# One block for the whole input projection of a hybrid decoder layer, with its guests handing memory over by semaphores

## The reference

```python
h = rms_norm(x, norm_g)
proj = jnp.einsum('btd,dn->btn', h, w_in)            # 544 rows x 7964 columns
...
xp = jnp.concatenate([buf, cqk], axis=1)             # group C: short causal convolution
for j in range(CONV_W):
    acc = acc + xp[:, j:j + T] * c_conv_w[j]
qk_c = jax.nn.silu(acc)
...
hc, (C1, n1, m1) = mlstm_chunkwise(qc, kc, vc, gif[:, :, 0], gif[:, :, 1], C0, n0, m0)
```

## Time and profile before

| what | value |
|---|---|
| three runs | 1905.7, 1909.7, 1914.8 us |
| median | 1909.7 us |
| span of the profiled execution, first to last instruction | 1913.1 us |
| time of the profiled execution | not listed apart from its span |
| TensorE busy | 1684.6 us, 88% of the span |
| granted TensorE clock, mean | 0.942 of full |
| slots 66 to 127 with their results | about 458 to 998 us |

### The profile page before, as it was taken

The page is one execution under the profiler, slowest core; times in us unless marked ns, Lnnn a source line. Parts: engine busy times, 40 slices in busy tenths (PEclk is TensorE's granted clock), DMA queues, the critical chain, the costliest instruction groups (busy, mean ns, idle before and its releaser), DMA issues. The chain is left out here.

```text
span 1913.1 us, 39025 instructions
## 1 busy us (share of the span) xinstructions
PE 1684.6 (88%) x14897; PEld 1300.9 (68%) x14897; DVE 808.4 (42%) x1592; ACT 586.3 (31%) x1353; POOL 103.8 (5%) x166
## 2 busy tenths in 40 slices
PE   6999998998998899999978887888888888369998
PEld 5888888776777677777556756666666666157776
DVE  4221222352266432334425654466455565374221
ACT  4321112231223121221115213455445455262110
POOL 3000000151000000000001000000000000020000
PEclk9999999998999999999897878999999999779999
DMA  6465555684422314124146515999999999193343
GB/s 210 154 200 184 173 188 159 220 292 127 157 70 91 110 51 127 56 83 119 47 140 238 171 41 183 358 358 384 372 384 373 374 364 378 53 332 88 122 158 115
DMA packets 218112, 373.28 MB, mean 195 GB/s; under 512 B 41917, under 2 KB 122254, under 8 KB 216614
## 3 DMA queue, kind: packets, MB, share of 16 engines
q1 hardware_dynamic: 214390, 359.24, 55.0%
q0 software_dynamic: 3248, 9.44, 1.5%
q10 hardware_dynamic: 288, 2.10, 0.3%
HBM read 334.27 MB, written 40.69 MB: 196 GB/s over the span
## 5 line engine op out<-in xcount | busy, mean ns | idle before, releaser
L370 PE MATMUL pj_ps<-pj_whi,pj_xhi 128*128 128x512 f32 (+1 forms) x1024 | 417.9, 408 | 5.9 <-PEq L86 5.9
L371 PE MATMUL pj_ps<-pj_wlo,pj_xhi 128*128 128x512 f32 (+1 forms) x1024 | 402.7, 393 | 0.0
L372 PE MATMUL pj_ps<-pj_whi,pj_xlo 128*128 128x512 f32 (+1 forms) x1024 | 401.4, 392 | 0.0
L288 DVE TENSOR_TENSOR pj_wlo<-pj_w,pj_whi 128x1024 fp32r<-128x1024 f32 (+1 forms) x128 | 156.2, 1221 | 461.1 <-ACT pj_whi L246 459.8
L246 ACT ACTIVATE pj_whi<-pj_w 128x1024 fp32r<-128x1024 f32 (+1 forms) x128 | 132.4, 1034 | 522.9 <-DMA pj_w<-in_w_in 521.5
L370 PEld LDWEIGHTS pj_ps<-pj_whi,pj_xhi 128*128 128x128 f32 x1024 | 198.3, 194 | 67.6 <-issue 30.9
L372 PEld LDWEIGHTS pj_ps<-pj_whi,pj_xlo 128*128 128x128 f32 x1024 | 198.0, 193 | 40.8
L371 PEld LDWEIGHTS pj_ps<-pj_wlo,pj_xhi 128*128 128x128 f32 x1024 | 198.8, 194 | 34.3
L1589 ACT ACTIVATE da_kT<-da_tp 128x512 f32<-128x512 f32 x200 | 119.2, 596 | 168.4 <-PE da_tp L1470 155.7
L1676 DVE COPY da_kT<-da_tp 128x512 f32<-128x512 f32 x128 | 88.5, 691 | 73.2 <-PE da_tp L1470 72.8
L3116 PE MATMUL ou_ps<-ou_whi,ou_mhi 128*128 128x512 f32 x256 | 104.7, 409 | 6.5 <-DVE ou_wlo L3040 6.5
(11 more groups left out here) (531 smaller groups left out, 2284.8 us busy)
## 6 DMA issues: line engine op xcount, KB each, us to landing
at_early_a<-in_cache_a_kv SPq DMA_DIRECT2D x128, 512.0 KB, 6.4
da_pa<-in_cache_a_kv SPq DMA_DIRECT2D x128, 512.0 KB, 6.7
pj_w<-in_w_in SPq DMA_DIRECT2D x120, 512.0 KB, 4.6
px_pages<-in_cache_b_kv SPq DMA_DIRECT2D x256, 128.0 KB, 2.5
at_early_b<-in_cache_b_kv SPq DMA_DIRECT2D x128, 128.0 KB, 6.5
da_pb<-in_cache_b_kv SPq DMA_DIRECT2D x128, 128.0 KB, 6.8
ou_w<-in_w_out SPq DMA_DIRECT2D x32, 512.0 KB, 4.3
proj<-pj_out SPq DMA_DIRECT2D x52, 256.0 KB, 5.6
```

The source lines that it names most:

```text
L288: dve.tensor_tensor(self.wlo[:, r, :, 0:n], self.w[:, r, :, 0:n], self.whi[:, r, :, 0:n], ALU.subtract).then_inc(self.wlo_ready, 1)
L370: pe.matmul(acc, hi, high, start=kc == 0, stop=False)
L371: pe.matmul(acc, hi, low, start=False, stop=False)
L372: last = pe.matmul(acc, lo, high, start=False, stop=kc == KC - 1)
```

## The change

The four blocks become one. `project` becomes the class `Opening`, whose `program` runs all 128 slots. The function `guests` strings the guests' generators together: when the beats of one segment are over, what is left of that guest is written out in one piece at the first turn of the next segment, and the next guest's turn 1 follows in the same turn. `Lease` is a stage that hands its semaphores to its owner: its memory is given back when it closes, but it clears nothing and has no barrier. Semaphores are cleared once, where the stage "pj" closes. In the place of the barriers come waits: `room` (norms stored, pages used) before the convolution's first loads and its first VectorE work, `k_copied` before the prompt part's loads and masks, and on GpSimd the landing of the prompt part's last stores before the sample part's masks. Last, the prompt part's SyncE, TensorE, ScalarE and VectorE streams start four turns later (`LEAD = 4`), except for four small copies on VectorE, so that its 72 turns are 76; and the sample part's `START` goes from 8 to 14.

```diff
+class Lease(Stage):
+    def __init__(self, nc, name, owner):
+        super().__init__(nc, name)
+        self.owner = owner
+    def sem(self, name):
+        return self.owner.sem(f"{self.name}_{name}")
...
@@ Opening.program (each engine; here SyncE) @@
                 for g in range(end):
                     a.sp_slot(sp, g)
+                part = guests(segments, "sp", sp)
+                for g in range(end, a.SLOTS):
+                    a.sp_slot(sp, g)
+                    beats(a, part, g)
+                for _ in part:
+                    pass
+                a.sp_end(sp)
...
-def hosted(nc, host, first, last, guest):
...
+def beats(host, part, g):
+    for _ in range(4 if g % host.NP < host.NP - 1 else 0):
+        next(part, None)
+
+def guests(segments, engine, eng):
+    for guest, first, last in segments:
+        part = {"sp": guest.sp, "pool": guest.pool, "act": guest.act, "dve": guest.dve, "pe": guest.pe}[engine](eng)
+        for _ in range(4 * sum(1 for g in range(first, last) if g % Projection.NP < Projection.NP - 1)):
             next(part, None)
+            yield
+        for _ in part:
+            pass
...
@@ Convolve @@
+    def room(self, eng):
+        for t in range(5):
+            eng.wait_ge(self.before.norms.stored[t], 48)
+        eng.wait_ge(self.host.pages_used, 8 * DB)
...
+        self.room(sp)
         sp.dma_start(self.old[32:36, :], d.c_conv_w).then_inc(self.w_loaded, 16)
...
+        self.room(dve)
         step(dve.memset(self.xp[:, :, 0:3], 0.0))
...
@@ PromptMemory @@
-    HEADBEATS, UNITBEATS = 15, 7
+    LEAD, HEADBEATS, UNITBEATS = 4, 15, 7
...
+        for _ in range(self.LEAD):
+            yield
+        sp.wait_ge(self.before.k_copied, 5)
         for t in range(5):
             sp.wait_ge(self.host.stored[t], (16 if t < PT else 64) * 10)
...
     def pool(self, pool):
+        pool.wait_ge(self.before.k_copied, 5)
...
     def pe(self, pe):
-        for _ in range(3):
+        for _ in range(self.LEAD + 3):
             yield
...
     def act(self, act):
-        for _ in range(3):
+        for _ in range(self.LEAD + 3):
             yield
...
         step(dve.tensor_copy(k.gates_s[:, 1, :], k.gate_f[:, SEQ:ROWS]))
+        for _ in range(self.LEAD):
+            yield
         dve.wait_ge(self.zeroed, 5)
...
@@ SampleMemory @@
-    START = 8
+    START = 14
...
     def pool(self, pool):
+        pool.wait_ge(self.before.out_stored, 16 * 7)
+        pool.wait_ge(self.before.h_stored, 16 * len(self.before.UNITS))
...
@@ stages @@
-            project(nc, d, k, host, 66)
-            with Stage(nc, "ml") as c:
+            with Lease(nc, "px", s) as g:
+                opening = Opening(nc, d, k, host, g)
+            with Lease(nc, "ml", s) as c:
...
-                    with Stage(nc, "cv") as g:
-                        hosted(nc, host, 66, 90, Convolve(nc, d, k, host, g))
-                    with Stage(nc, "mp") as g:
-                        hosted(nc, host, 90, 112, PromptMemory(nc, d, k, host, g))
-                with Stage(nc, "md") as g:
-                    hosted(nc, host, 112, 128, SampleMemory(nc, d, k, host, g))
+                    with Lease(nc, "cv", s) as g:
+                        conv = Convolve(nc, d, k, host, opening, g)
+                    with Lease(nc, "mp", s) as g:
+                        prompt = PromptMemory(nc, d, k, host, conv, g)
+                with Lease(nc, "md", s) as g:
+                    sample = SampleMemory(nc, d, k, host, prompt, g)
+            opening.program(66, [(conv, 66, 90), (prompt, 90, 112), (sample, 112, 128)])
```

More of the change, by code:

```diff
@@ L527, in dve, with __init__, program @@
             dve.tensor_scalar(ss[0:rows, t, 16:22], ss[0:rows, t, 16:22], 1.0 / HEAD, None, ALU.mult).then_inc(self.summed, 1)
-def project(nc, d, k, a, end):
-    with Stage(nc, "px") as s:
+class Opening:
+    def __init__(self, nc, d, k, a, s):
+        self.nc, self.d, self.k, self.a = nc, d, k, a
         a.pages = s.sb("pages", [P, 3, 4, 2 * HEAD])
         a.table = s.sb("table", [1, DB * PAGES], I32)
[L535 to L550, removed]
+        self.x = s.sb("x", [P, 5, D])
+        self.sq = s.sb("sq", [P, D])
+        self.ssq = s.sb("ssq", [P, 8])
+        self.rms = s.sb("rms", [P, 8])
+        self.gain = s.sb("gain", [P, KC])
+        self.xg = s.sb("xg", [P, 3, 4, P])
+        self.x_loaded = s.sems("x_loaded", 5)
+        self.gain_loaded = s.sem("gain_loaded")
+        self.made = s.sem("made")
+        self.z_zeroed = s.sem("z_zeroed")
+        self.turned = s.sem("turned")
+        self.xg_ready = s.sem("xg_ready")
+        self.xhi_ready = s.sem("xhi_ready")
+        self.squared = s.sem("squared")
+        self.rooted = s.sem("rooted")
+        self.norms = Norms(nc, d, k, a, self.x, self.sq, s)
+    def program(self, end, segments):
+        nc, d, k, a = self.nc, self.d, self.k, self.a
+        x, sq, ssq, rms, gain, xg = self.x, self.sq, self.ssq, self.rms, self.gain, self.xg
+        x_loaded, gain_loaded, made, z_zeroed = self.x_loaded, self.gain_loaded, self.made, self.z_zeroed
+        turned, xg_ready, xhi_ready = self.turned, self.xg_ready, self.xhi_ready
+        squared, rooted, norms = self.squared, self.rooted, self.norms
         parts = [(t, q) for t in range(5) for q in range(4)]
@@ L603, in _ @@
                 norms.pool(pool)
+                for _ in guests(segments, "pool", pool):
+                    pass
             @block.scalar
@@ L629, in _ @@
                     norms.act(act, g)
+                part = guests(segments, "act", act)
+                for g in range(end, a.SLOTS):
+                    a.act_slot(act, g)
+                    beats(a, part, g)
+                for _ in part:
+                    pass
             @block.vector
@@ L663, in _ @@
                         dve.wait_ge(a.rstd_ready, 1)
+                part = guests(segments, "dve", dve)
+                for g in range(end, a.SLOTS):
+                    a.dve_slot(dve, g)
+                    beats(a, part, g)
+                for _ in part:
+                    pass
             @block.tensor
@@ L683, in _ @@
                     a.pe_slot(pe, g)
+                part = guests(segments, "pe", pe)
+                for g in range(end, a.SLOTS):
+                    a.pe_slot(pe, g, part)
+                for _ in part:
+                    pass
 class Blocks:
@@ L1807, in _ @@
                     dve.tensor_copy(oo[:, 1 + x // 2, 4 * (x % 2):4 * (x % 2) + 4, :], src).then_inc(out_dve, 1)
-def hosted(nc, host, first, last, guest):
-    def beats(part, g):
-        for _ in range(4 if g % host.NP < host.NP - 1 else 0):
-            next(part, None)
[L1820 to L1861, removed]
+def beats(host, part, g):
[5 more added lines that the diff above has]
+        for _ in range(4 * sum(1 for g in range(first, last) if g % Projection.NP < Projection.NP - 1)):
+            next(part, None)
+            yield
+        for _ in part:
+            pass
 class Convolve:
@@ L1868, with __init__ @@
     N = len(JOBS)
-    def __init__(self, nc, d, k, host, s):
-        self.d, self.k, self.host = d, k, host
+    def __init__(self, nc, d, k, host, before, s):
+        self.d, self.k, self.host, self.before = d, k, host, before
         self.banks = host.ps[5:8]
@@ L2418, with __init__ @@
     V = HEAD + 1
-    START = 8
-    def __init__(self, nc, d, k, host, s):
-        self.d, self.k = d, k
+    START = 14
+    def __init__(self, nc, d, k, host, before, s):
+        self.d, self.k, self.before = d, k, before
         self.bx, self.by, self.bz = host.ps[5], host.ps[6], host.ps[7]
@@ L3177, in stages @@
                 k.gates_s = c.sb("gates_s", [HC, 2, NS])
-                with Stage(nc, "mi") as m2:
+                with Lease(nc, "mi", s) as m2:
                     k.qkT = m2.sb("qkT", [P, 8, ROWS])
```

## The result

| | before | after |
|---|---|---|
| median, 20 runs each | 1908.1 us | 1916.9 us |
| ratio after / before, 95% interval | | 1.0045 (1.0030 to 1.0061) |
| span of the profiled execution | 1913.1 us | 1917.9 us |
| TensorE busy, granted clock | 1684.6 us, 0.942 | 1685.1 us, 0.943 |
| slots 89 to 111 | 231.3 us | 238.3 us |

By the ratio the kernel is 8.6 us slower (0.45%, interval 5.7 to 11.6). That is just inside the 0.5% that I called no change, but the interval leaves out 1. The forecast was +17.4: its direction held, and about half of its size. One of the changed kernel's 20 executions took 2023.9 us at a mean clock of 0.816 and is left out of the ratio.

What follows compares the result with a forecast made beforehand. TensorE, busy 88% of the span, was taken as the bound. Barriers -7.1, LEAD +8.9, handover +8.9 and rest of the sample part +6.7 sum to +17.4 us, on the median 1909.7: 1927 us; range 1904 to 1938.

Steps and rivals of the forecast that it cites:

- the barriers' terms of 7.1: Three inner barriers and the final clear removed: 1.8, 2.95 with 1.7 of clock, and 0.6, together 7.1 us saved.
- The handover's stop: At the third barrier, slot 112 starts 1.1 us after TensorE ends slot 111 instead of 4.05: 2.95 us back.
- The 0.6 for the final clear: At the end, one semaphore clear with its barrier goes; worth 0 to 0.9 us, taken as 0.6.
- LEAD in slots 90 to 111: Prompt part four turns later: idle +6.1, clock +2.8, together +8.9 us; bounds -7.7 and +14.
- the 1.7 at turns 19 and 20: Slot 94: query scaling and two key weights wait behind the split; two stops of some 0.8, sum 1.7 us.
- The handover: Slot 112: late-landing prompt stores delay state and weight loads; idle +5.4, clock +3.5, together +8.9 us; bounds 0 and +13.
- 1.7 of clock behind the third barrier: Stretch 850 to 860 us: 3.4 us at 1.2 GHz, 1.7 us of work lost, which removing the barrier gives back.
- turn 26: Slot 118, sample part: key weights and weighing fall behind the split, a stop of 1.0 us.
- the rest of the sample part, six turns later: Turn 26 1.0, slot 120 0.5, slot 126's late weights 3.5 and clock 1.7: together +6.7 us; bounds 0 and +11.
- Leads do what a lead can: Rival: guest turns find their data ready because weights arrive earlier; -15 us, 1895 us; chance 0.10.
- In part: Rival: handover costs but VectorE's turns keep clear of splits, or the other way round; 1911 us, within 0.5%; chance 0.28.
- the same rule: VectorE is in order, so even-slot guest turns run after the split, past +6.4 us, though TensorE asks at +1.4 to +5.6.

Runs made afterwards that it cites:

- kernel 1: The changed kernel with LEAD 0 and START 8 as before the change, also called block only: ratio 0.9954 to the kernel before, median 1897.6 us.
- kernel 9: The changed kernel without its two stores of n_p, run once: 1904.2 us; SyncE's wait at the handover 2.6 us instead of 7.7.
- kernels 2 and 3: The changed kernel with START 8 and LEAD still 4: ratio 1.0047 to before; the changed kernel with LEAD 0 and START still 14: 0.9946.
- kernels 4 and 7: The changed kernel with VectorE's guest turns before the split in even slots from 90: 0.9914; that plus both store moves: 0.9872 (ratios to before).
- kernel 11: The kernel before, barriers kept, with VectorE's guest turns ahead of the low split in even slots from 90: ratio 0.9869, median 1885.9 us.

## Why the prediction was half right

The forecast's terms can be set beside the two profiles, place by place (the barriers' terms of 7.1 stand where they belong):

| place | forecast | the two profiles |
|---|---|---|
| slots 64 to 88 | -0.9 | -3.7 |
| slots 89 to 111, with the handover's stop | +5.0 | +7.0 |
| slots 112 to 126 | +13.9 | +7.8 |
| slot 127 to the next stage's first matmul | -0.6 | +0.1 |
| sum | +17.4 | +11.2 |

These are two single executions. Slot 64 starts at 445.5 us before and at 440.3 after, though the programs do the same work up to there; the thirteen kernels' profiles have it between 440 and 447. And the profile before is a slow one: its span of 1913.1 fits only the run of 1914.8 us, the slowest of the twenty (a run's time is some 1.8 us above its span).

**The barriers: -7.1 forecast, -8.8 measured** by kernel 1 (interval -5.3 to -12.0). The handover's stop is 1.16 in every kernel with one block, as worked out (1.1). The 0.6 for the final clear wasn't there: from the start of slot 127 to the next stage's first matmul it is 19.1 us before and 19.2 after, and TensorE ends that time in a wait for that stage's rows.

**LEAD in slots 90 to 111: the steps right, the sum right with some luck.** The slots' stops forecast and found: 4.3 gone, yes; end of 92, 2.9 and 2.62; mp_w in 96 and 104, 4.5 together and 3.4; end of 102, 2.4 and 2.95; end of 110, 2.4 and 2.54. Of the 1.7 at turns 19 and 20 only 0.3 was there. Added up, idle time came out at about +4 and not +6.1, and the loss of clock at +6.8 and not +2.8; the two misses cancel in part. Executions of the same slots differ, too: with LEAD 4 and this order stage 1 took 238.3, 229.8, 235.8 and 230.4 us (and 235.6 with the stores in slot 110). The mean of the four, 233.6, stands against a forecast of 231.3 - 0.9 - 2.95 + 8.9 = 236.4.

**The handover: the mechanism right, the times within about a microsecond.** Stores landed at T + 13.0 (forecast 11.8), weights of 116 were asked for at T + 24.8 (25.8), stops of 3.04, 0.2 and 4.47 (4.2, 0.7 and 4.3). The 6.7 us for the landing held (7.7), and kernel 9 shows it is the stores of single elements. The figure of about 2 us that the prediction sets beside it stands in the Trainium skill (DMA: Bandwidth & Descriptors, Anatomy of one DMA) for transfers that GpSimd issues; these are SyncE's, so the comparison says less than it seems to.

**The step that failed is the size of the two stage 2 terms: +8.9 for the handover and +6.7 for the rest, less 1.7 of clock behind the third barrier, 13.9 in all, measured +7.8.** Idle time was forecast at +10.4 and was +8.4 (the handover +4.0 and not +5.4; slot 126 stopped 2.2 and not 3.5; turn 26 took 2.0, not 1.0). The larger part is the clock, forecast at +3.5 (two stops of 2.6 against one of 1.7, another 1.7 at slot 126, less 1.7 behind the third barrier). It came out at 0.0, 8.5 us lost in both. After lost what the prices ask and a little more: 5.1 us at the handover's two stops, 1.7 each behind the 2.0 and the 2.2. But before had lost 5.1 us that the prediction didn't count, behind the stop of 1.1 that it priced at nothing:

```profile
938.60:948.80 10.20, 10.20 (x18) 4.66 (x17) 6.39 (x10) 0.00 (x0) 0.00 (x0) 0.50 0.01 2
```

Of the seven other kernels that kept this stop, at 1.1 to 1.4 us, one (block only) has 3.4 us at 1.2 GHz behind it and the others none; after has the same work at 955 to 965 with a clock of 1.00. So this loss is that execution's and not the program's.

The ratios, which don't hang on one execution, point the same way. From block only to the changed kernel, which is LEAD, handover and rest together, the forecast was +24.5 and the ratios say +17.4 (0.9954 to 1.0045). Of this stage 1 has about 10 (233.6 less 223.1, the mean of the two kernels with one block, LEAD 0 and this order), which leaves about 7 for stage 2 where the forecast had 15.6. That is my estimate from six executions. And the term for "the rest of the sample part, six turns later" was all cost, while START 14 as a whole changed nothing that can be told (kernels 2 and 3). How much of the miss is idle time and how much is clock in a usual execution stays open.

**The rivals.** "Leads do what a lead can" needed splits that end before +3 in even slots; they end at +6.0 to +7.1. "In part" came nearest in time (1911 against 1916.9), but by luck: every turn it wanted clear of the splits stopped, save two.

**What I hadn't seen** is what the same rule offered: if guests are late because they stand behind a split, the split can stand behind the guests. That is 25 us, nearly three times the barriers. The rule was in the rows of before; I used it only to price the change.

## What to carry to other kernels

When an in-order engine serves two customers, put the instruction that waits for a transfer behind the ones whose data are there, as long as it still meets its own due time; look for an engine that is idle just ahead of an instruction in front of ready work. Where a host's pattern is two slots long, a shift of its guest by one slot puts odd-slot work into even slots: four turns of "slack" cost 18 us here. (A shift by two slots was not run.) A barrier's stop is worth its length less the wait that stands behind it: of 4.05 us at the handover 1.16 stayed. A queue's wait for a landing belongs where nothing urgent stands behind it. And charge the clock by a mean over executions: with the same instructions and like stops this kernel's stage 1 took 230 us in one and 238 in another.

## What the runs showed of the hardware

- With two stores of 256 single elements of 4 bytes each among them, the prompt's last stores had landed 7.7 us after the last issue, 6.8 us after their last packet had ended; without these two, four stores of 64 KB and one of eight elements took 2.6 us from the last issue and 0.5 us from the last packet.
- The granted clock often fell to 1.2 GHz behind stops of 1.1 us and more, for 3.4 to 10.2 us, but not behind each: with the same stops, each within a microsecond, 34 us of stage 1 were at 1.2 GHz in one execution and 17 in another. Stage 1 with a single stop of 1.4 or 1.6 us had 1.00 over 212 us (kernels 4 and 7), but with none over 0.9 before its last barrier (kernel 11) it has 742.0 to 745.4 at 1.2 GHz, behind a stop of 0.4.
